# The S5 core of a fused block: four stages with a hand-made recurrence against one stage in four chunks with a scan instruction

## Chip, core and metric
One core of one Trainium2 chip. The metric is the device time of one execution, in microseconds (us); less is better. The engines are TensorE (PE: matmuls; PEld: its weight loads), VectorE (DVE), ScalarE (ACT), GpSimd (POOL) and SyncE (SP), which here only issues DMAs. They run their own instruction queues and meet at semaphores.

## What is computed
A gated delta net, a dense FFN, an S5 mixer, a mixture of experts and two attention layers on 512 tokens of width 1024. The change lies in the S5 mixer alone:
```python
def s5_mixer(x, w_in, lam_re, lam_im, log_dt, b_re, b_im, c_re, c_im, d_skip, w_glu):
    u = (x @ w_in).astype(f32)
    lam = lax.complex(lam_re, lam_im); dt = jnp.exp(log_dt)[:, None]
    a_bar = jnp.exp(lam * dt)
    b_bar = ((a_bar - 1.0) / lam)[..., None] * lax.complex(b_re, b_im)
    # h_t = a_bar * h_(t-1) + b_bar u_t   for 64 groups of 16 features, 64 complex states each
    # y_t = real(c h_t) + d_skip * u_t
    hid = jax.nn.gelu(y, approximate=False)
    val, gate = jnp.split(hid @ w_glu, 2, axis=-1)
    return val * jax.nn.sigmoid(gate)
```
(The two comment lines stand for the reference's chunked associative scan.)

## The kernel before
Names: P is 128, STEP 8 tokens, NJ = 64 blocks of 8 tokens, PAIRS = 32 pairs of groups (one of the pair in partitions 0 to 63, the other in 64 to 127), GC = 16 features of a group. The recurrence runs over the 64 blocks; inside a block of 8 tokens everything is matrices. A `Stage` gives each engine its own list of instructions; the next stage begins when all engines are through.

`s5_u` (`s5_project`, L1951): the projection x @ w_in in eight feature groups f. ScalarE rounds weight tiles (`split_hi`), VectorE makes their low parts (`split_lo`, L3858, two inputs from SBUF), and TensorE multiplies in three passes (`three_pass`, L263 to L267); ScalarE copies each group out (L1984), stores it to DRAM (L1989), and SP loads it back with tokens turned into blocks (`load_turned`, L1948, 8 DMAs a group, into `u_blk`). Beside that VectorE builds the matrices from inputs to block states (`powers`: 48 operations of 512 elements, L2085 to L2096, into `p_t`), three powers ahead of the low part of tile 2, two ahead of that of tile 3, three behind. GpSimd has nothing.

`s5_tables` (L2014): 64 transposes of `p_t` (L2036), copied to `into`, then the block inputs (L2045), copied to `e_all`.

`s5_scan` (L2167): VectorE steps eight blocks of eight with one complex product a step (L2266 to L2270), then carries between the eight (L2277 to L2281), then adds the carried part (L2294 to L2298). GpSimd clears three mixing buffers (L2319) and makes powers of the pole (`block_powers`, L2154 to L2164, two-input operations while VectorE steps). SP loads the output matrices `q_re`, `q_im` (L2305, 16 DMAs), TensorE makes the responses inside a block (`lags`, L2208/L2209, each group by itself on 64 rows), ScalarE copies them (L2241), and SP places each shifted copy of them in the mixing matrices `mix` with 8 DMAs a quarter (L2313, 32 in all); TensorE applies them (`within`, L2220), and keeps itself busy (`keep_busy`, L194) in between.

`s5_outputs` (L2334): the states times `q` (L2356), added by VectorE to the rest (L2366). `s5_gelu` (L2370): y turned back (L2389), d_skip * u added by VectorE (L2405), gelu on ScalarE (L2419), rounding (L2422) and low part (L2399), with 18 kept-busy calls on TensorE (two passes of 384 columns each). Then `s5_glu` multiplies by w_glu in its own stage; its first four weight tiles are loaded behind `s5_scan`, into the ring that `mix` used.

## Time and profile before
| | |
|---|---|
| median of 3 runs | 2594.73 us (2594.63 to 2598.16) |
| the profiled execution | span 2590.5 us from first to last instruction; instructions 41313 |
| busy: PE, DVE, ACT, POOL | 2477.6 us (96%), 1739.2 (67%), 1051.9 (41%), 589.9 (23%) |
| mean granted clock of TensorE | 0.991 of full |
| S5 part | `s5_u` 836.5 to 886.4, core and gelu to 981.2, then `s5_glu` |

A profile row gives an engine, a line of the kernel, the operation, written tile <- read tiles, partitions x elements and a count. "idle before" with an arrow is time that the engine stood still just before and who ended it. The granted clock is a share of 2.4 GHz; at 0.5 TensorE runs at 1.2 GHz. Kept-busy matmuls count as busy.

### The profile page before, as it was taken

The numbers are of one execution on the slowest core, as the hardware profiler recorded it, in microseconds if no ns is written. First come the engines' busy times: TensorE is split into PE (matmuls) and PEld (weight loads), VectorE is DVE, ScalarE is ACT, GpSimd is POOL, SyncE is SP. The second block draws the span as 40 slices with busy tenths as digits, with TensorE's granted clock in tenths as the row PEclk, the third lists the DMA queues.
The fourth block names the chain that finished last, engine by engine and source line by source line (L and its number), as shares of the span: only waits on it lengthen the run. The fifth ranks groups of instructions, "written<-read, shape, count | busy, mean of one in ns | idle before, by whom it ended". The sixth has DMA issues, their size and how long they took to land. (4 is left out here: it accounts for less than half of the span.)

```text
span 2590.5 us, 41313 instructions
## 1 busy us (share of the span) xinstructions
PE 2477.6 (96%) x15961; PEld 2036.9 (79%) x15961; DVE 1739.2 (67%) x2869; ACT 1051.9 (41%) x1561; POOL 589.9 (23%) x447
## 2 busy tenths in 40 slices
PE   8998999999999989899999999998999999999998
PEld 6788887788887768899999999886776576767566
DVE  6945656467676784576666767676687567487667
ACT  4443233321212333355555555533344443344453
POOL 2404321430230020052333432440024001024001
PEclk9999999999999999999999999999999999999999
DMA  4321002346654252267776777853221211332121
GB/s 155 98 83 35 2 3 65 124 156 237 212 182 148 76 166 84 91 219 229 254 240 224 252 236 231 271 184 125 86 74 60 76 66 57 109 94 70 33 82 65
DMA packets 259968, 339.98 MB, mean 131 GB/s; under 512 B 24928, under 2 KB 217952, under 8 KB 259232
## 3 DMA queue, kind: packets, MB, share of 16 engines
q1 hardware_dynamic: 251840, 315.52, 37.6%
q0 software_dynamic: 4512, 15.99, 1.8%
q10 hardware_dynamic: 3456, 6.29, 0.8%
q8 instruction: 106, 1.74, 0.3%
q14 instruction: 54, 0.44, 0.1%
HBM read 318.63 MB, written 16.52 MB: 129 GB/s over the span
## 5 line engine op out<-in xcount | busy, mean ns | idle before, releaser
L3020 PE MATMUL ps<-x_feat_r,moe_w_hi 128*128 128x384 f32 x1408 | 405.1, 361 | 0.6 <-DVE x_feat_r L3132 0.6
L2545 DVE TENSOR_TENSOR moe_w_lo<-ring,moe_w_hi 128x2048 fp32r<-128x2048 f32 x144 | 316.1, 2196 | 126.8 <-ACT moe_w_hi L2540 126.6
L3023 PE MATMUL ps<-x_feat_r,moe_w_lo 128*128 128x192 f32 x1408 | 354.0, 251 | 0.0
L2540 ACT ACTIVATE moe_w_hi<-ring 128x2048 fp32r<-128x2048 f32 x144 | 254.8, 1770 | 93.5 <-PE ps L263 76.2
L3023 PEld LDWEIGHTS ps<-x_feat_r,moe_w_lo 128*128 128x128 f32 x1408 | 269.2, 191 | 0.3
L3020 PEld LDWEIGHTS ps<-x_feat_r,moe_w_hi 128*128 128x128 f32 x1408 | 264.3, 188 | 1.7 <-issue 1.4
L267 PE MATMUL ps<-x_free_r,ring_r 128*128 128x512 f32 x496 | 195.6, 394 | 0.0
L266 PE MATMUL ps<-ring_r,x_feat_r 128*128 128x256 f32 (+2 forms) x576 | 185.1, 321 | 0.0
L263 PE MATMUL ps<-x_feat_r,ffn_w_hi 128*128 128x512 f32 x352 | 139.3, 396 | 1.2 <-DVE ffn_w_lo L2488 1.2
L267 PE MATMUL ps<-x_feat_r,ffn_w_lo 128*128 128x512 f32 x352 | 139.4, 396 | 0.0
L266 PE MATMUL ps<-x_free_r,ffn_w_hi 128*128 128x512 f32 x352 | 138.5, 393 | 0.0
L2540 ACT ACTIVATE ffn_w_hi<-ring 128x2048 fp32r<-128x2048 f32 (+1 forms) x35 | 61.8, 1768 | 169.4 <-PE ps L263 100.8
L4061 ACT ACTIVATE s_sb<-s_sb,att_small 128x512 f32<-128x512 f32 (+3 forms) x128 | 71.9, 562 | 133.3 <-DVE att_small L4053 133.1
L266 PEld LDWEIGHTS ps<-ring_r,x_feat_r 128*128 128x128 f32 x576 | 110.0, 191 | 7.8
L194 PE MATMUL ps<-cst 128*128 128x384 f32 x266 | 95.4, 506 | 17.8 <-PEq L175 15.7
L267 PEld LDWEIGHTS ps<-x_free_r,ring_r 128*128 128x128 f32 x496 | 93.2, 188 | 21.2
L3068 ACT ACTIVATE moe_cross<-ps 128x384 f32<-128x384 f32 (+1 forms) x96 | 44.4, 462 | 150.5 <-PE ps L3023 150.5
L263 PE MATMUL ps<-x_feat_r,acc_r 128*128 128x512 f32 x256 | 102.2, 399 | 0.0
L267 PE MATMUL ps<-x_feat_r,ring_r 128*128 128x512 f32 x256 | 101.7, 397 | 0.0
L266 PE MATMUL ps<-x_free_r,acc_r 128*128 128x512 f32 x256 | 101.5, 397 | 0.0
L3251 POOL TENSOR_TENSOR moe_hid_hi<-moe_prod,cst 128x384 fp32r<-128x384 f32 (+1 forms) x48 | 54.3, 1131 | 190.2 <-DVE moe_prod L3195 190.2
L4329 POOL TENSOR_TENSOR sq<-c_all 128x512 f32<-128x512 f32 x16 | 19.7, 1234 | 341.7 <-ACT c_all L3937 341.7
(661 smaller groups left out, 6407.1 us busy)
## 6 DMA issues: line engine op xcount, KB each, us to landing
ring<-in_moe_w SPq DMA_DIRECT2D x120, 1024.0 KB, 5.5
ring<-in_w_in SPq DMA_DIRECT2D x32, 1024.0 KB, 5.3
ring<-in_ffn_w SPq DMA_DIRECT2D x30, 1024.0 KB, 7.4
ring<-in_ada_t SPq DMA_DIRECT2D x48, 512.0 KB, 4.3
ring<-in_gdn_w_in SPq DMA_DIRECT2D x12, 1024.0 KB, 6.0
ring<-in_moe_w SPq DMA_DIRECT2D x24, 512.0 KB, 3.8
ring<-in_s_w_glu SPq DMA_DIRECT2D x8, 1024.0 KB, 5.6
ring<-in_w_out SPq DMA_DIRECT2D x8, 1024.0 KB, 6.2
```

The costliest lines, as they stand in the source:

```text
L194: prog.nc.tensor.matmul(prog.ps[:, bank, 0:3 * P], prog.ident, prog.cst, start=True, stop=True)
L263: m = nc.tensor.matmul(out, lh, rh, start=first, stop=False)
L266: nc.tensor.matmul(out, lh, rl, start=False, stop=False)
L267: return nc.tensor.matmul(out, ll, rh, start=False, stop=last)
L2540: self.prog.nc.scalar.activation(self.flat(self.hi, j % SPLITS, j), self.raw(j), ACT.Copy).then_inc(self.hi_done, 1)
L2545: self.prog.nc.vector.tensor_tensor(self.flat(self.lo, j % SPLITS, j), self.raw(j), self.flat(self.hi, j % SPLITS, j).bitcast(F32), ALU.su ...
L3020: mm = nc.tensor.matmul(out, wh[:, k, cs], both[:, k, :], start=(k == 0), stop=False)
L3023: mm = nc.tensor.matmul(out[:, 0:SLOTS], wl[:, k, cs], xg[0][:, k, :], start=False, stop=(k == KD - 1))
L3068: nc.scalar.activation(cross_of(c, which), half(c, which, 1), ACT.Copy).then_inc(cross_copied, 1)
L3251: nc.gpsimd.tensor_tensor(hi, src, prog.ones[:, 0:1].unsqueeze(2).to_broadcast([P, len(ms), SLOTS]), ALU.mult).then_inc(hi_ready, 1)
L4061: self.nc.scalar.activation(x, x, ACT.Exp, bias=self.small[:, u % 4, 1:2], scale=self.heads[h][3], accum_out=self.small[:, u % 4, 2:3]).th ...
L4329: m = nc.gpsimd.tensor_tensor(sq[:, 0 if first else 1, :], c_all[:, k, :], c_all[:, k, :], ALU.mult)
```

## The change
- `s5_tables`, `s5_scan`, `s5_outputs` and `s5_gelu` become one stage, `s5_core`, that goes through the 32 pairs in four chunks of eight.
- The recurrence is turned into a frame that rotates with the pole's angle: what is left is a real decay, done by `tensor_tensor_scan` (two instructions of 128x512 a chunk). The rotations, for 63 blocks and 32 pairs, and the decays are made by GpSimd during `s5_u`, by doubling. VectorE turns the inputs into the frame and the states out of it (`scan`).
- The response matrices of both groups of a pair come out of one matmul over 128 rows, with weights that are zero outside their own group (`lag_w`, written by GpSimd). GpSimd adds the skip term to them, and SP places them with 16 DMAs a chunk, one set for each group, in four mixing buffers.
- `within` and `states` add up in PSUM; gelu reads PSUM. The projected features stand in a ring of three.
- The four weight tiles of `s5_glu` are loaded inside `s5_core`, one behind each chunk's output.

Cut to what matters, with the removed functions (printed above) left out:
```diff
-GSTEP = 8
+SC = 4
+SQ = PAIRS // SC
+QUAD = SQ // 2
+LR = 2 * GC
...
+        for part, table in enumerate((mag, cos, pow_im)):
+            m = nc.vector.tensor_copy(s5.pole[:, part, :], table[:, STEP, :])
+        link(m)
...
+class S5Room:
...
+    U_RING = 3
...
+        raw = new("raw", [P, 2 * PAIRS * (STEP + 1) * GC])
+        n = 2 * PAIRS * P
+        self.p_t = raw[:, 0:n].rearrange("p (r q i c) -> p r q i c", r=2, q=PAIRS, c=GC)
+        self.tmp = raw[:, n:n + 2 * PAIRS * GC].rearrange("p (r q c) -> p r q c", r=2, c=GC)
...
+        self.rot = new("rot", [P, 2, PAIRS, NJ])[:, :, :, :]
+        self.decay = new("decay", [P, PAIRS, NJ])[:, :, :]
+        work = new("work", [P, 4, 2 * SQ * NJ])
+        self.turn = [work[:, i, :].rearrange("p (q j) -> p q j", q=PAIRS) for i in range(4)]
+        self.e, self.t, *self.h = (work[:, i, :].rearrange("p (r q j) -> p r q j", r=2, q=SQ) for i in range(4))
...
+        self.into = [x.rearrange("p k n -> p (k n)").rearrange("p (q n) -> p q n", n=P) for x in (prog.x_feat, prog.x_free)]
+        self.hid = [self.u_ring[:, n].rearrange("p i j -> p (i j)") for n in range(self.U_RING)]
...
+def rotations(nc, link, s5, room):
+    tt = nc.gpsimd.tensor_tensor
+    rot, turn = room.rot, room.turn
+    nc.gpsimd.memset(rot[:, 0, :, 0], 1.0)
+    nc.gpsimd.memset(rot[:, 1, :, 0], 0.0)
+    for part in range(2):
+        nc.gpsimd.tensor_copy(rot[:, part, :, 1], s5.pole[:, 1 + part, :])
+    link(nc.gpsimd.tensor_copy(room.decay, s5.pole[:, 0, :].unsqueeze(2).to_broadcast([P, PAIRS, NJ])))
+    link(nc.gpsimd.memset(room.decay[:, :, 0], 0.0))
+    n = 1
+    while n < NJ - 1:
+        m = min(n, NJ - 1 - n)
+        shape = [P, PAIRS, m]
+        re, im = (rot[:, part, :, 1:m + 1] for part in range(2))
+        top_re, top_im = (rot[:, part, :, n:n + 1].to_broadcast(shape) for part in range(2))
+        t = [x[:, :, 0:m] for x in turn]
+        tt(t[0], re, top_re, ALU.mult)
+        tt(t[1], im, top_im, ALU.mult)
+        tt(t[2], re, top_im, ALU.mult)
+        link(tt(t[3], im, top_re, ALU.mult))
+        tt(rot[:, 0, :, n + 1:n + m + 1], t[0], t[1], ALU.subtract)
+        link(tt(rot[:, 1, :, n + 1:n + m + 1], t[2], t[3], ALU.add))
+        n += m
...
+def s5_project(prog, name, s5, room):
...
+        def u_feat(f):
+            return room.u_ring[:, f % room.U_RING]
...
+                if f >= room.U_RING:
+                    act.wait_ge(u_stored[f - room.U_RING], 16)
...
+            def powers(taus):
+                real_powers(prog, dve, link, bbar, pow_re, pow_im, by_step[0], taus, room.tmp)
+                imaginary_powers(prog, nc.vector, room.tmp, link, bbar, pow_re, pow_im, by_step[1], taus)
+            proj.split_lo(dve, 0)
+            proj.split_lo(dve, 1)
+            powers(BACK[0:3])
+            proj.split_lo(dve, 2)
+            powers(BACK[3:5])
+            proj.split_lo(dve, 3)
+            powers(BACK[5:])
+        @st.gpsimd
+        def _(pool):
+            rotations(nc, linker(pool, pool_link), s5, room)
...
+def s5_core(prog, name, s5, room):
...
+    jobs = [(b, r, 8 * b + 4 * half) for b in range(SC) for r in range(2) for half in range(2)]
+    T_BANKS = (2, 3, 4, 5, 6, 7)
+    by_dve = [i < 8 and i % 2 == 1 for i in range(len(jobs))]
...
+                pe.wait_ge(prog.u_landed[b], 2 * 16 * STEP)
+                for r in range(2):
+                    for n in range(SQ):
+                        q = b * SQ + n
+                        for gp in range(2):
+                            m = nc.tensor.matmul(ps[TOKENS[gp], E_BANK + r, n * NJ:(n + 1) * NJ],
+                                                 into[r][:, q, TOKENS[gp]], u_blk[:, PAIRS * gp + q, :], start=True, stop=True)
+                m.then_inc(e_ready, 1)
...
+                rows = lag_rows(s // 2)
+                for n in range(QUAD):
+                    q = s * QUAD + n
+                    out = ps[rows, LAG_BANK + s % 2, n * P:(n + 1) * P]
+                    for r, x in enumerate((q_re, q_im)):
+                        m = nc.tensor.matmul(out, room.lag_w[r][:, q, :], flat_steps(x[:, q, 0:STEP, :]),
+                                             start=(r == 0), stop=(r == 1))
...
+            def within(b):
+                pe.wait_ge(placed[b], 32 * STEP)
...
+            def states(b):
+                pe.wait_ge(h_ready, b + 1)
...
+                pe.wait_ge(y_copied, 2 * b + 2)
...
+            turn_tables(0)
+            turn_tables(1)
+            inputs(0)
+            turn_tables(2)
+            turn_tables(3)
+            lags(0)
+            lags(1)
+            inputs(1)
+            lags(2)
+            lags(3)
+            within(0)
+            states(0)
+            inputs(2)
+            lags(4)
+            lags(5)
+            turn_back(0)
+            within(1)
+            states(1)
+            inputs(3)
+            lags(6)
+            lags(7)
+            turn_back(1)
+            within(2)
+            states(2)
+            turn_back(2)
+            within(3)
+            states(3)
+            pe.wait_ge(e_read, SC)
+            keep_busy(prog, E_BANK, 4)
+            turn_back(3)
+            keep_busy(prog, E_BANK, 10)
...
+            def finish(b):
+                act.wait_ge(e_ready, 3 + b // 2)
+                for gp, f in enumerate(features(b)):
+                    n = 2 * b + gp
+                    hid = room.hid[n % room.U_RING]
+                    if n >= room.U_RING:
+                        act.wait_ge(lo_done, n - room.U_RING + 1)
...
+                        act.wait_ge(y_turned, 2 * b + half + 1)
+                        nc.scalar.activation(by_half[:, half],
+                                             ps[:, TURN_BANK + half, :].rearrange("p (i g j) -> p g i j", g=2, j=NJ)[:, gp], ACT.Gelu
+                                             ).then_inc(gelu_done, 1)
+                    act.wait_ge(gelu_done, 2 * n + 2)
+                    nc.scalar.activation(prog.x_hi[:, f, :], hid, ACT.Copy).then_inc(hi_done, 1)
...
+            def scan(b):
+                e, t, h = room.e, room.t, room.h[b % 2]
+                shape = [P, 2, SQ, NJ]
+                cos, sin = (rot[:, part, chunk(b), :] for part in range(2))
+                dve.wait_ge(e_ready, b + 1)
+                raw = ps[:, E_BANK:E_BANK + 2, :].rearrange("p r (q j) -> p r q j", j=NJ)
+                tt(e, raw, cos.unsqueeze(1).to_broadcast(shape), ALU.mult)
+                tt(t[:, 0], raw[:, 1], sin, ALU.mult)
+                m = tt(t[:, 1], raw[:, 0], sin, ALU.mult)
+                m.then_inc(e_read, 1)
+                dve.wait_ge(e_read, b + 1)
+                tt(e[:, 0], e[:, 0], t[:, 0], ALU.add)
+                link(tt(e[:, 1], e[:, 1], t[:, 1], ALU.subtract))
+                decay = room.decay[:, chunk(b), :].rearrange("p q j -> p (q j)")
+                for r in range(2):
+                    m = nc.vector.tensor_tensor_scan(t[:, r].rearrange("p q j -> p (q j)"), decay,
+                                                     e[:, r].rearrange("p q j -> p (q j)"), 0.0, ALU.mult, ALU.add)
+                link(m)
+                if b >= 2:
+                    dve.wait_ge(y_ready, 2 * (b - 2) + 2)
+                tt(e, t, cos.unsqueeze(1).to_broadcast(shape), ALU.mult)
+                late, early = slice(1, NJ), slice(0, NJ - 1)
+                tt(h[:, 0, :, late], t[:, 1, :, early], sin[:, :, early], ALU.mult)
+                link(tt(h[:, 1, :, late], t[:, 0, :, early], sin[:, :, early], ALU.mult))
+                tt(h[:, 0, :, late], e[:, 0, :, early], h[:, 0, :, late], ALU.subtract)
+                link(tt(h[:, 1, :, late], e[:, 1, :, early], h[:, 1, :, late], ALU.add))
+                dve.sem_inc(h_ready, 1)
...
+            tt(skip, mask.unsqueeze(1).to_broadcast(shape), s5.d_skip.unsqueeze(2).to_broadcast(shape), ALU.mult
+               ).then_inc(skip_ready, 1)
+            copy_tables(0)
+            copy_tables(1)
+            scan(0)
+            scan(1)
+            scan(2)
+            split_lo(0)
+            scan(3)
+            for b in range(1, SC):
+                split_lo(b)
...
+                pool.wait_ge(lag_copied, s + 1)
+                rows, qs = lag_rows(s // 2), slice((s % 2) * QUAD, (s % 2 + 1) * QUAD)
+                nc.gpsimd.tensor_tensor(room.lag[rows, qs, 0:GC], room.lag[rows, qs, 0:GC], skip[rows, qs, :], ALU.add
+                                        ).then_inc(skip_added, 1)
+                pool.wait_ge(skip_added, s + 1)
+            for r in range(2):
+                m = nc.gpsimd.memset(room.lag_w[r], 0.0)
+            link(m)
+            for gp in range(2):
+                rows = TOKENS[gp]
+                for r in range(2):
+                    link(nc.gpsimd.tensor_copy(room.lag_w[r][rows, :, gp * GC:(gp + 1) * GC], s5.bbar[rows, r]))
+            pool.sem_inc(wide_ready, 1)
+            pool.wait_ge(skip_ready, 1)
+            for b in range(SC):
+                zero(b)
+                add_skip(2 * b)
+                add_skip(2 * b + 1)
...
+            sp.wait_ge(prog.u_last_stored, 16)
+            load_turned(prog, sp, u_blk, KD - 1)
             for s in range(NS):
+                sp.wait_ge(turned, min(8 + 4 * (s // 2), len(jobs)))
+                for r, dst in enumerate((q_re, q_im)):
+                    sp.dma_start(dst[:, quad(s), :, :], prog.q_dram[:, r, quad(s)]).then_inc(q_landed[s], 16)
+            for b in range(SC):
+                sp.wait_ge(zeroed, b + 1)
+                sp.wait_ge(skip_added, 2 * b + 2)
+                for i in range(STEP):
+                    n = (STEP - i) * GC
                     for gp in range(2):
+                        at = LR * b + GC * gp
+                        sp.dma_start(mix[b][i * GC:(i + 1) * GC, :, gp, i * GC:], room.lag[at:at + GC, :, 0:n]
+                                     ).then_inc(placed[b], 16)
+            for b in range(SC):
+                sp.wait_ge(y_ready, 2 * b + 2)
+                W.load(sp, W.issued)
+                W.issued += 1
```

## Rows read from the trace of the kernel before
**Rows 1.** Stretches; busy us of PE, PEld, DVE, ACT, POOL; granted clock; DMA.
```profile
836.50:842.10 5.60, 5.58 (x11) 3.81 (x12) 4.08 (x5) 3.99 (x5) 0.00 (x0) 0.50 0.02 4
842.10:886.40 44.30, 42.60 (x186) 34.69 (x185) 36.82 (x51) 12.26 (x10) 0.00 (x0) 1.00 0.29 82
886.40:981.20 94.80, 79.97 (x1060) 65.82 (x1060) 75.47 (x130) 41.83 (x61) 20.00 (x27) 0.98 0.46 127
923.90:927.40 3.50, 3.50 (x35) 2.43 (x32) 3.31 (x10) 1.18 (x2) 0.00 (x0) 0.51 0.57 92
981.20:988.90 7.70, 6.21 (x29) 6.22 (x30) 4.79 (x5) 3.99 (x5) 0.00 (x0) 0.56 0.46 157
```
**Rows 2.** Timeline of PE, scan to glu: start, length.
```profile
922.92 1.09 PE L2220 MATMUL ps<-ring,s_ublk 128*64 128x128 f32 x16 [2.11 <-DMA ring<-ring]
...
942.73 1.97 PE L2220 MATMUL ps<-ring,s_ublk 128*64 128x128 f32 x32 [1.96 <-DMA ring<-ring]
...
967.73 11.78 PE L194 MATMUL ps<-cst 128*128 128x384 f32 x36
982.69 0.58 PE L263 MATMUL ps<-s_glu_hi,x_feat_r 128*128 128x256 f32 x1 [3.18 <-DVE ring_r L242]
```
**Rows 3.** Groups of one line: duration in ns min/median/max, first and last start.
```profile
L2036 PE MATMUL ps<-cst,s_he x64: 272/273/302, 886.6 to 893.5; 128*128 128x128 f32 x64
L2045 PE MATMUL ps<-s_ublk,s_into x256: 222/222/270, 893.7 to 901.2; 128*64 128x64 f32 x128
...
L2419 ACT ACTIVATE s_hid<-s_yfeat x8: 1122/1130/1164, 966.6 to 978.5; 128x512 f32<-128x512 f32 x8
L2422 ACT ACTIVATE x_feat_r<-s_hid x8: 629/630/633, 967.8 to 979.6; 128x512 fp32r<-128x512 f32 x8
...
909.69 1.06 ACT L2241 ACTIVATE ring<-ps 16x512 f32<-16x512 f32 x2 [8.12 <-PE ps L2209]
```
**Rows 4.** The timeline of DVE, PE and ACT in `s5_u`.
```profile
865.71 2.29 DVE L3858 TENSOR_TENSOR ring_r<-ring,acc_r 128x2048 fp32r<-128x2048 f32 x1 [0.25 <-ACT acc_r L3850]
873.44 0.39 PE L263 MATMUL ps<-x_feat_r,acc_r 128*128 128x512 f32 x1
879.52 0.69 DVE L2096 TENSOR_TENSOR s_he<-s_u_tmp 128x512 f32<-128x512 f32 x1
884.74 1.03 ACT L1984 ACTIVATE s_ufeat<-ps 128x512 f32<-128x512 f32 x1 [4.44 <-PE ps L267]
```
**Rows 5.** GpSimd's operations alone: two lines' groups, two rows of its timeline.
```profile
L1480 POOL TENSOR_TENSOR acc<-acc,gdn_ms 128x512 f32<-128x512 f32 x2 | 2.1, 1064 | 0.9 <-DVE gdn_ms L1486 0.9
L1482 POOL TENSOR_TENSOR acc<-acc,gdn_z 128x512 f32<-128x512 f32 x2 | 2.5, 1267 | 0.2
...
211.90 2.35 POOL L1679 TENSOR_TENSOR gdn_z<-gdn_z,gdn_par 128x1024 f32<-128x1024 f32 x1 [85.18 <-POOLq L175]
922.93 0.39 POOL L2164 COPY x_free<-x_free 128x256 f32<-128x256 f32 x1
```
**Rows 6.** Timelines of DVE and POOL, alone and against each other.
```profile
24.54 2.33 DVE L953 SCALAR_TENSOR_TENSOR gdn_ktok<-gdn_conv_padded,gdn_taps,gdn_ktok 128x512 f32<-128x512 f32 x3
71.58 4.00 DVE L953 SCALAR_TENSOR_TENSOR gdn_ktok<-gdn_conv_padded,gdn_taps,gdn_ktok 128x512 f32<-128x512 f32 x3
71.51 1.29 POOL L866 TENSOR_TENSOR gdn_z_hi<-gdn_vtok,gdn_z_hi 128x512 fp32r<-128x512 f32 x1 [3.11 <-ACT gdn_z_hi L914]
72.76 1.49 POOL L862 TENSOR_TENSOR gdn_vtok<-gdn_q 128x512 f32<-128x512 f32 x1
...
918.65 0.83 DVE L2269 TENSOR_TENSOR x_free<-x_free,s_he 128x512 f32<-128x512 f32 x1
```
**Rows 7.** SP's DMA groups: placement, turned loads and the latter's landing.
```profile
L2313 SPq DMA_DIRECT2D ring<-ring x32: 559/618/2565, 912.7 to 940.7; - x32
L1948 SPq DMA_DIRECT2D s_ublk<-u_turn x64: 303/431/1360, 849.4 to 891.2; - x64
...
DMA to landing us min/median/max: 1.7/1.9/2.9
```

546 lines of the change are left out of this document (196 added, 350 removed).

## The prediction
> **What bounds the kernel now.** I read the views in this order. The page's first part: TensorE is busy for 96% of the span. That share hides two kinds of time that a change of the S5 part can win: idle stretches, and matmuls that only keep the clock up. So I cut the span into stretches [rows 1]: the projection `s5_u` with its start at half clock (836.5 to 842.1) and the rest of it to 886.4, the four stages behind it (tables, scan, outputs, gelu) from 886.4 to 981.2, and the first 7.7 us of the gated projection behind them, again at 0.56 of the full clock. In the 94.8 us of the four stages TensorE shows 80.0 us busy, but that includes 34 kept-busy calls (68 passes of L194, of which the last 36 take 11.78 us [rows 2]); no engine is the limit of all four stages. In the scan stage VectorE goes through its hand-made recurrence (75.5 us of VectorE in the stretch [rows 1]), while TensorE waits for the placed matrices again and again [rows 2]; at the end ScalarE's gelu (1.12 us for each of eight features, then 0.63 us of rounding [rows 3]) is what TensorE idles for. The reader should see a chain that changes engine from stage to stage with nothing overlapped across the stage borders. In `s5_u`, by contrast, TensorE is the limit: VectorE has done its last power at 880.2, TensorE goes on to about 884.7, and ScalarE's copy behind it ends at 885.8 [rows 4], so VectorE has 6 us to spare.
>
> **Part 1, the rotations on GpSimd in `s5_u`.** GpSimd is idle there before (0.00 us busy [rows 1]). The change puts one copy of 128x2048 and 36 two-input operations there: six for each m of 1, 2, 4, 8, 16, 31, on 32m elements. Four of six read an operand that repeats along the innermost axis; the nearest row took 1.04 us for 512 elements, two full operands 1.27 us for 512 and 2.35 us for 1024 [rows 5]. That is 2.1 ns an element for two full operands over a start of 0.19 us, and 1.66 ns with a repeated one. Port time (I count 0.05 us of the start): m=31 (992 elements) 4x1.70 + 2x2.13 = 11.1 us; m=16 5.9; m=8 3.1; m=4, 2, 1 together 3.3; the copy, by 0.39 us for 256 elements [rows 5], 2.4. Sum 25.8 us.
> Is it hidden? GpSimd alone would have 49 us for it. But VectorE's operations there all read two inputs from SBUF, and where both do that, three of L953 take 4.00 us against L866 and L862 on GpSimd, and 2.33 us without them [rows 6]. 1.67 us of the about 2.1 us that the two hold the port (0.9 and 1.15 us, from the end of the VectorE instruction that they wait for) come on top, 80%. For small operations less: VectorE's 0.69 us become 0.83 beside GpSimd's operations of 128 elements (0.32 us of port time), 44%, since VectorE's own start hides the rest [rows 6]. So 0.8 x (11.1+5.9+3.1+2.4) + 0.4 x 3.3 = 19.3 us: VectorE ends at 880.2 + 19.3 = 899.5. TensorE meets it earlier: the low part of tile 3 was made at 865.7 to 868.0 [rows 4] and is needed at 873.4 [rows 4]; behind 30 slowed operations it comes at about 882, so TensorE stands still for some 9 us and ends the last two groups near 894 to 897. That is before 899.5, so it adds nothing more. The stage ends 899.9 instead of 886.4: **+13.5 to +14 us**, I take +14. Below: 0 if the port isn't shared by these operations; above: +20 if all 25.8 us come through.
> The Trainium skill, page "SBUF — State Buffer", section "Who interferes with whom", says that a VectorE instruction with two SBUF inputs and a GpSimd instruction that reads SBUF exclude each other for their whole length: "the other fully blocks". By that rule, the trace agrees [rows 6], and the whole sum is +20 instead of +14, the end at 2596. It speaks against this change, for GpSimd's work looks free in a table of busy shares.
>
> **Part 2, four stages become one.** The work of TensorE stays: 64 transposes in 6.9 us, the inputs' 256 passes in 7.6 us, each pass of 128 columns 0.055 us where two halves of the array run side by side (32 in about 1.8 us) [rows 2, 3]. Only the lag matmuls change form: 64 of them over all 128 rows with nothing beside them, two passes of 0.109 us each (the transposes' pace), 1.75 us for four pairs. VectorE's recurrence, which filled the scan stage, becomes four calls of scan(b): two operations of 1024 elements (about 1.22 us each, between 0.69 for 512 and 2.29 for 2048 [rows 4]), eight of 512 at 0.61 to 0.69, sum 7.7 us, and two of the scan instruction, which the trace doesn't show: 0.69 us as an ordinary two-input operation, up to 2 us when an element depends on the last. I take 1.2. It matters little: the first two calls are wanted 27 and 41 us into the stage and are done at 17 and 27, the last two begin when their inputs are there and have 17 us each. Only from 3 us an instruction on does VectorE set the end.
> A sentence on a page: the Trainium skill, "DVE: opcode table, instruction layouts, handler registers and perf-mode slots", section "Datapath and trigger behaviour", says that this instruction runs at half throughput; by it each is 1.2 us, 4 us in all beyond a two-input operation, none of it on the path.
> What sets the end is the chain lags, copy, skip addition, placement, within. The placement was 32 DMAs (median 0.62 us of SP each, 256 pieces) and becomes 64 of 128 pieces; the turned loads have 128 pieces and take 0.43 us, begun 0.475 us apart [rows 7]. I take 0.51 us between two, 8.2 us for a chunk's 16, and 2.2 us for the last to land (the turned loads: 1.9 in the middle, 2.9 at most [rows 7]). Working it out from the stage's start:
> (a) turn 16 tables 7.0, inputs(0) 1.9, lags(0), (1) 3.5: 12.4; TensorE comes from a pause, so the clock is at its lower level (1.2 GHz) for the first few us, +1.6: 14.0.
> (b) ScalarE's copy 0.53 (half of the old pair's 1.06 [rows 3]), GpSimd's addition of 64 elements about 0.4 (0.19 + 64 x 2.1 ns, and its semaphore): 15.1. SP has issued its 16 loads of q by then.
> (c) 16 placements 8.2 and landing 2.2: 25.5. TensorE did inputs(1), lags(2), (3) and then idles 5 us.
> (d) within 1.8, states 3.6, inputs 1.9, lags 3.5, turning back 0.9, within 1.8, states 3.6, inputs 1.9, lags 3.5: 22.5, to 48.0; half clock behind the idle 5 us, +2.2: 50.2.
> (e) copy, addition 1.1, 16 placements 8.2, landing 2.2: 61.7; 7.2 us of TensorE's work (chunks 1 and 2) lie under it.
> (f) within(3) 1.8, states(3) 3.6, 4 kept-busy calls 2.6 (8 passes at 11.78/36 = 0.327 us), turning back 0.9, 10 calls 6.5: 15.4, and 1.7 for the clock: 78.8.
> The last ten calls outlast the gelu of the last chunk (four of 0.57, two roundings of 0.63, one low part of 0.69: about 5 us), which they cover. On SP nothing else waits behind the placements but the four loads of the next weights; three go out at about 58 us, the last behind states(3) at 67, and the first tile is there long before it is needed.
> So 78.8 us stand for 94.6: **-15.8**. Skip terms, table copies and the wait on the ring of three features cost nothing: ScalarE has 12 us of work in 44 in `s5_u` [rows 1], and the stored feature it waits for is two groups old. If the ring's cover were gone it would be the store's 2.2 us.
>
> **Part 3, the start of the next stage.** Before, TensorE's last kept-busy pass ended at 979.5 and the first matmul came 3.18 us later [rows 2], and the 7.7 us around it ran at 0.56 [rows 1], which costs 3 us. Now the kept-busy calls themselves end the stage, and the pause is 1.7 us. A pause of 1.96 us before 942.73 was followed by full clock, one of 2.11 us before 922.92 by 3.4 us at the lower level [rows 1, 2]. So I take **-3**; 0 is the other end.
>
> **Sum.** 14 - 15.8 - 3 = -4.8 us on the profiled span of 2590.5; the median of the runs, 2594.73, lies 4.2 us above that span, and nothing changes around it. 2594.73 - 4.8 = 2590.
>
> **The rivals.** (A) GpSimd's work is hidden. For it: GpSimd has 49 us for 26, and some VectorE inputs repeat along the innermost axis, as in no row here. Against: [rows 6]. The 14 us fall away: 2576. (B) The placement on SP sets a slower beat. The old 32 were begun between 912.7 and 940.7 [rows 7], 0.9 us apart with their waits; if the 64 go at 0.9 too, the 32 on the path add 32 x 0.39 = 12.5 us: 2602. From 0.66 us between two the kernel is no faster than before, from 0.82 it is slower by what can be measured. For it: each chunk's matrices move as many small pieces as before, and the first meet the q loads. Against: 0.475 us apart for the same count of pieces. (C) The port passes on everything: +6, 2596. (D) The clock does not fall in the core: -5.9, 2584; against it, two pauses of 3 and 5 us. (E) The scan instruction doesn't do what it is for and takes 4 us, so VectorE becomes the bound: +9, 2599; against it, no two-input row is near this.
>
> **How the numbers follow.** Forecast 0.38 (its own range 2585 to 2595), A 0.15, B 0.20, C 0.12, D 0.10, E 0.05. A measurement can tell about 0.2%, 5.2 us, from no change: faster is below 2589.5, slower above 2599.9. Faster: A, D and half of the forecast's chance, 0.44. Same: the other half and C, 0.31. Slower: B and E, 0.25. The range goes from just under A to B with a little more, 2574 to 2604.
>
> **What would show it.** In `s5_u`: L2085-like operations of 0.69 us grow to over 2 us beside GpSimd's widest ones, and TensorE waits some 9 us for VectorE at the sixth group; if they stay at 0.69, A holds. In the core: TensorE's wait for the placement DMAs, about 5 us before the first within and 3 us before the last; starts of placement DMAs 0.5 us apart; scan instructions near 1.2 us; the granted clock at 1.0 at the start of the gated projection. The prediction is wrong if the stage behind `s5_u` starts before 890, or the core takes under 72 or over 86 us.

## The result and the profile after

The changed kernel takes 2600.5 us in the median of nine runs against 2594.6 for the kernel before, a ratio of 1.0026 with a 95% interval of 1.0015 to 1.0038: slower by 3.9 to 9.9 us, best value 6.7. The forecast was 2590, a little faster; the time lies in its range (2574 to 2604), its direction is wrong: 4.8 us less were forecast. The profiled execution of the changed kernel took 2603.47 us with a span of 2601.8.

Windows of the changed kernel, cut where its stages and waits are (columns as in [rows 1]):

```profile
839.00:842.00 3.00, 2.94 (x5) 1.25 (x5) 2.30 (x2) 2.96 (x5) 2.84 (x8) 0.50 0.04 8
842.00:876.30 34.30, 34.23 (x144) 27.84 (x144) 33.75 (x31) 10.05 (x9) 33.52 (x30) 0.96 0.25 72
876.30:891.40 15.10, 0.00 (x1) 0.03 (x1) 14.96 (x7) 1.02 (x1) 12.73 (x6) 0.58 0.18 46
891.40:906.60 15.20, 13.30 (x48) 10.45 (x49) 11.67 (x18) 2.14 (x2) 0.03 (x1) 0.86 0.11 32
906.60:935.50 28.90, 18.78 (x256) 17.57 (x256) 23.48 (x34) 8.76 (x16) 12.20 (x13) 0.90 0.66 205
935.50:961.00 25.50, 25.46 (x392) 23.94 (x392) 14.67 (x19) 8.71 (x14) 4.19 (x4) 0.91 0.30 48
961.00:975.30 14.30, 7.81 (x115) 6.93 (x114) 9.19 (x12) 8.49 (x15) 0.92 (x1) 0.96 0.28 44
975.30:993.80 18.50, 18.42 (x132) 13.80 (x132) 1.39 (x2) 4.54 (x8) 0.00 (x0) 0.85 0.71 228
993.80:1002.00 8.20, 6.60 (x55) 6.60 (x56) 4.79 (x5) 4.00 (x5) 0.00 (x0) 1.00 0.43 147
```

TensorE has three stretches with long idle times: all of 876.3 to 891.4 in the projection, and in the core (906.6 to 993.8) some 10 of the first 28.9 us and 6.5 of the 14.3 us before 975.3. The timeline of TensorE says what ended each (start, length, instruction, in brackets the idle time before it and its releaser):

```profile
891.40 0.77 PE L263 MATMUL ps<-x_feat_r,acc_r 128*128 128x512 f32 x1 [15.17 <-DVE ring_r L3895]
...
906.62 3.68 PE L2181 MATMUL ps<-cst,s_raw 128*128 128x128 f32 x32 [1.91 <-PEq L175]
...
935.54 3.68 PE L2228 MATMUL ps<-ring,s_ublk 128*64 128x128 f32 x32 [8.21 <-DMA ring<-acc]
939.15 4.13 PE L2240 MATMUL ps<-s_raw,s_work 64*64 64x128 f32 x64
...
949.86 1.97 PE L2228 MATMUL ps<-ring,s_ublk 128*64 128x128 f32 x32
...
975.28 3.68 PE L2228 MATMUL ps<-ring,s_ublk 128*64 128x128 f32 x32 [5.03 <-DMA ring<-acc]
...
995.40 0.38 PE L263 MATMUL ps<-s_glu_hi,x_feat_r 128*128 128x256 f32 x1 [1.68 <-DVE ring_r L242]
```

L2228 is `within`, L2240 `states`, L2181 the turning of the tables. From such rows of both kernels the two spans compare like this (us):

| stretch | before | after | difference | forecast |
|---|---|---|---|---|
| start of the span to the first kept-busy matmul of `s5_u` | 836.5 | 839.1 | +2.5 | 0 |
| `s5_u`, to the first turned table | 50.1 | 67.6 | +17.5 | +14 |
| four stages, or the core, to the last kept-busy pass | 92.9 | 87.1 | -5.8 | |
| pause before the gated projection | 3.2 | 1.7 | -1.5 | |
| (these two together, forecast) | | | -7.3 | -15.8 |
| first 200 matmuls of the gated projection | 26.7 | 24.0 | -2.7 | -3 |
| the rest | | | +1.3 | 0 |

The S5 part alone comes to +7.5 us, which lies inside what the medians show (3.9 to 9.9). The first and the last line are not the change's: `s5_u` began between 836.0 and 839.6 us in the executions of all kernels below, which are alike up to there, and what follows the start of the gated projection took between 1602.9 us (experiment 10) and 1611.7 us (experiment 6) in the changed kernels. So every experiment is read from its own stages first and from its median second. One of the five executions of experiment 3 ran at a granted clock of 0.636 and took 3525.8 us, and is left out of its ratio.

### The profile page after: what moved, and what is told of

It is laid out like the page before. It is cut to its first block and busy times, and to the rows that moved or that the text cites. A ratio compares the mean times of both kernels' runs of the same rounds, so it can differ in the third digit from the quotient of the medians.

```text
span 2601.8 us, 40981 instructions
## 1 busy us (share of the span) xinstructions
PE 2470.5 (95%) x15793; PEld 2034.8 (78%) x15793; DVE 1732.9 (67%) x2804; ACT 1040.5 (40%) x1553; POOL 635.1 (24%) x480
## 5 line engine op out<-in xcount | busy, mean ns | idle before, releaser
L263 PE MATMUL ps<-x_feat_r,acc_r 128*128 128x512 f32 x256 | 102.5, 400 | 15.2 <-DVE ring_r L3895 15.2
L194 PE MATMUL ps<-cst 128*128 128x384 f32 x226 | 83.6, 517 | 15.5 <-PEq L175 13.4
```

The lines of the kernel that those rows point to most:

```text
L194: prog.nc.tensor.matmul(prog.ps[:, bank, 0:3 * P], prog.ident, prog.cst, start=True, stop=True)
L263: m = nc.tensor.matmul(out, lh, rh, start=first, stop=False)
```

## The experiments

Every kernel was compared with the kernel before on the same chip, whose median was 2594.4, 2595.3, 2594.9 and 2595.9 us in the four groups of runs. "Projection" is `s5_u` from its first kept-busy matmul to the core's first turned table (before 50.1, after 67.6), "core" from there to the last kept-busy pass (after 87.1).

**1. No rotations.** The table of rotations is filled with 1 and 0; the work of the other engines stays.

```diff
-    n = 1
-    while n < NJ - 1:
...
-        n += m
+    nc.gpsimd.memset(rot[:, 0], 1.0)
+    nc.gpsimd.memset(rot[:, 1], 0.0)
```

> This kernel is the changed one without the 36 two-input operations of the rotations on GpSimd: the table is filled with 1 and 0 by two memsets, so the states come out in a wrong frame; everything else stays, the copy of the decay too. Theory P (the 17.5 us that the projection stage grew, 67.6 us between its first kept-busy matmul and the core's first transpose where it was 50.1, are VectorE and GpSimd excluding each other): the stage goes back to 50 to 51 us, VectorE's power operations back to 0.69 us, the whole to 2600.5 - 17 = 2583.5. Rival R (the stage grew because of something else in it, such as the ring of three stored features or the moved low part of tile 3): GpSimd's absence changes little, the stage stays above 60 us, the whole within 3 us of 2600. Both: the core stays at 87 us.

Measured: 2582.2 us, ratio 0.9952 (0.9936 to 0.9969). The projection takes 50.2 us, the core 86.9. The whole growth of the projection is the rotations' doing, and with it gone the rest of the change is worth 12 us.

**2. The rotations alone, in the kernel before.**

```diff
+            @st.gpsimd
+            def _(pool):
+                rotations(nc, linker(pool, pool_link), pole, room)
```

> This kernel is the one before with the same rotations (36 two-input operations, the copy of 2048 elements) on GpSimd in its projection stage, on operands of the same shapes, into memory that nothing reads. Theory P: the stage grows by 17 us (50.1 to about 67), TensorE stops some 15 us before the last quarter of the weights, the whole is 2594.6 + 17 = 2612. Rival R: GpSimd's work is not what does it, the stage stays within 3 us of 50.

Measured: 2614.7 us, ratio 1.0070 (1.0049 to 1.0091), so +18 us, as much as the first experiment took away. The projection takes 67.5 us, and TensorE stops where it does in the changed kernel, for the same wait:

```profile
888.54 0.77 PE L263 MATMUL ps<-x_feat_r,acc_r 128*128 128x512 f32 x1 [15.27 <-DVE ring_r L3897]
...
903.66 0.52 PE L2075 MATMUL ps<-cst,s_he 128*128 128x128 f32 x3 [1.89 <-PEq L175]
...
1003.16 0.38 PE L263 MATMUL ps<-s_glu_hi,x_feat_r 128*128 128x256 f32 x1 [3.19 <-DVE ring_r L242]
```

In the projection it is 17.4 us less there and 17.4 us more here: the cost hangs on GpSimd's work and on nothing else of the change. The four stages behind it took 96.3 us here and 92.9 in the kernel before, which no experiment explains. The last row shows one thing more: the pause before the gated projection is 3.19 us, as in the kernel before (3.18), and yet the next 7.7 us ran at a granted clock of 1.00 where they ran at 0.60 there; the first 200 matmuls took 24.0 us, as in the changed kernel.

**3. One operand in PSUM.** The same work on both engines; only where VectorE's operands live is changed.

```diff
-    pow_re, pow_im, bbar = s5.pw[:, 0], s5.pw[:, 1], s5.bbar
+    pow_re, pow_im = s5.pw[:, 0], s5.pw[:, 1]
+    bbar, first = (prog.ps[:, b:b + 2, :].rearrange("p r (q c) -> p r q c", c=GC) for b in (4, 6))
+    tmp = (first[:, 0], room.tmp[:, 1])
...
             proj.split_hi(act, 0)
+            for r in range(2):
+                nc.scalar.activation(bbar[:, r], s5.bbar[:, r], ACT.Copy).then_inc(moved, 1)
             proj.split_hi(act, 1)
```

> The changed kernel with the operand that all of VectorE's powers read (bbar) copied into two PSUM banks by two ScalarE copies, and the first of the two temporaries in PSUM too, so that each of the 48 power operations has one SBUF and one PSUM input; GpSimd's rotations stay. Theory P (only a VectorE instruction with two SBUF inputs excludes GpSimd): power operations stay near 0.7 us beside GpSimd, only the low parts of tiles 2 and 3 collide, the stage is 50 to 54 us instead of 67.6, the whole 2600.5 - 15 = 2585. Rival P' (any work of GpSimd on SBUF slows VectorE, wherever its operands are): power operations of 1.5 to 2.5 us beside the wide rotations as now, the whole within 3 us of 2600.

Measured: 2582.0 us, ratio 0.9941 (0.9922 to 0.9959); the projection takes 50.1 us. VectorE and GpSimd in the changed kernel, with the widest rotations beside the powers:

```profile
874.95 2.40 DVE L2103 TENSOR_TENSOR s_raw<-s_bbar,s_pow 128x512 f32<-128x512 f32 x1
877.38 2.27 DVE L2104 TENSOR_TENSOR s_raw<-s_raw 128x512 f32<-128x512 f32 x1
876.76 2.34 POOL L2006 TENSOR_TENSOR s_work<-s_rot 128x992 f32<-128x992 f32 x1
...
886.36 2.74 POOL L2010 TENSOR_TENSOR s_rot<-s_work 128x992 f32<-128x992 f32 x1
886.98 4.27 DVE L3895 TENSOR_TENSOR ring_r<-ring,acc_r 128x2048 fp32r<-128x2048 f32 x1
891.17 0.68 DVE L2093 TENSOR_TENSOR s_raw<-s_bbar,s_pow 128x512 f32<-128x512 f32 x1
```

and in this kernel:

```profile
867.74 0.70 DVE L2107 TENSOR_TENSOR ps<-ps,s_pow 128x512 f32<-128x512 f32 x1
868.35 0.68 DVE L2108 TENSOR_TENSOR s_raw<-ps,s_pow 128x512 f32<-128x512 f32 x1
869.79 3.44 DVE L3900 TENSOR_TENSOR ring_r<-ring,acc_r 128x2048 fp32r<-128x2048 f32 x1
...
867.27 1.93 POOL L2006 TENSOR_TENSOR s_work<-s_rot 128x992 f32<-128x992 f32 x1
...
871.03 3.98 POOL L2008 TENSOR_TENSOR s_work<-s_rot 128x992 f32<-128x992 f32 x1
```

The reader should see three things. In the changed kernel each of VectorE's 512-element operations lasts about as long as the GpSimd operation beside it (2.27 and 2.40 against 2.34), and is back at 0.68 as soon as GpSimd is done. With one input in PSUM the two engines run at their own speeds, 0.70 and 1.93. And where VectorE still reads two SBUF inputs, for the low part of a weight tile (L3900), the two collide as before: 3.44 instead of 2.29 there, 3.98 instead of 1.93 on GpSimd. So it is not GpSimd's activity that slows VectorE but two operands of VectorE in SBUF. The Trainium skill, page "SBUF — State Buffer", section "Who interferes with whom", says that a VectorE instruction with at most one SBUF input, outside its two-port modes, doesn't contend with GpSimd; the trace agrees, 0.70 us beside GpSimd's 1.93.

**4. Placements on two queues.**

```diff
-            for b in range(SC):
-                sp.wait_ge(zeroed, b + 1)
...
+            for b in range(SC):
+                place(sp, b, 0)
...
+            copy_lags(0)
+            copy_lags(1)
+            place(act, 0, 1)
+            copy_lags(2)
+            copy_lags(3)
+            place(act, 1, 1)
             copy_y(0)
```

`place(eng, b, gp)` waits for the chunk's memset and skip additions and issues its eight DMAs of group gp; chunks 2 and 3 likewise behind `copy_lags(5)` and `(7)`.

> The changed kernel with the placements of one of the two groups of each pair issued by ScalarE instead of SP, 8 of a chunk's 16 each; the same DMAs, pieces and bytes. Theory Q (the core is longer than forecast because SP begins a placement only every 0.645 us, 11 to 12 us a chunk with one longer one in it): a chunk is issued in about 6 us, TensorE's waits before the first and the last within shrink from 8.2 and 5.0 us to about 2.5 and 0, the core from 87 to 77 us, the whole to 2590. Rival Q' (what takes the time is the landing of many small pieces on the DMA engines): both waits stay within 2 us of what they are, and the landing times grow.

Measured: 2601.8 us, ratio 1.0024 (1.0010 to 1.0038), core 85.3: next to nothing, and neither theory holds throughout. A chunk was issued in 6.5 us, about as theory Q had it. But the first chunk's placements landed late, as rival Q' had it, and TensorE's wait before the first within was still 6.9 us; the last chunk's did not land late, and the wait for them was gone (line view of the placements in each stretch):

```profile
L2179 SPq DMA_DIRECT2D ring<-acc x8: 596/636/1146, 919.0 to 924.5; - x8
L2179 ACTq DMA_DIRECT2D ring<-acc x8: 622/638/1492, 919.0 to 924.9; - x8
...
DMA to landing us min/median/max: 4.7/6.3/7.0
```
```profile
L2179 SPq DMA_DIRECT2D ring<-acc x8: 586/613/1424, 958.8 to 964.4; - x8
...
DMA to landing us min/median/max: 1.9/2.7/3.4
```

And ScalarE, busy issuing for 6.6 us, came late with its copies: TensorE now waited for it, 4.50 us, before the turning back that precedes the last within.

```profile
970.06 1.94 PE L2264 MATMUL ps<-cst,acc 128*128 128x128 f32 x8 [4.50 <-ACT acc L2319]
971.93 3.28 PE L2237 MATMUL ps<-ring,s_ublk 128*64 128x128 f32 x32
```

The last chunk had been placed by 966.7, 7.9 us after its first issue (12.4 in the changed kernel). The issue time saved on SP was given back as a wait for ScalarE.

**5. All lags first.**

```diff
             inputs(1)
-            lags(2)
-            lags(3)
+            for s in range(2, NS):
+                lags(s)
             within(0)
             states(0)
             inputs(2)
-            lags(4)
-            lags(5)
             turn_back(0)
```

> The changed kernel with the lag products of chunks 2 and 3 (and ScalarE's copies of them) moved ahead of the first within, into the 8.2 us in which TensorE waits for the first placement; the same instructions otherwise. Theory Q (the rest of the core is paced by SP: 64 placement DMAs at 0.645 us with one longer one in each chunk, 0.70 us apart on the mean; they stop at 945 to 951 and 961 to 963 only because the lags of chunks 2 and 3 come late): SP issues all 64 in one run of 45 us from the first, within(3) starts 5.5 us earlier, and as TensorE pauses less, within and states run at full clock; the core from 87 to 80 us, the whole 2600.5 - 7 = 2593.5. Rival L (the placements are limited by landing on the DMA engines, which the denser issue doesn't help): landing times grow past 4 us in chunks 1 to 3 and the core stays within 2 us of 87.

Measured: 2594.4 us, ratio 1.0004 (0.9993 to 1.0015); core 80.6 us. SP's queue now holds one unbroken run of placements where the changed kernel's covers 51 us with two holes:

```profile
922.87 51.13 SPq L2454 DMA_DIRECT2D ring<-acc  x64
```
```profile
921.58 44.88 SPq L2446 DMA_DIRECT2D ring<-acc  x64
```
```profile
957.56 1.97 PE L2228 MATMUL ps<-ring,s_ublk 128*64 128x128 f32 x32 [2.90 <-DMA ring<-acc]
...
967.73 3.68 PE L2228 MATMUL ps<-ring,s_ublk 128*64 128x128 f32 x32 [2.71 <-DMA ring<-acc]
```

64 DMAs in 44.88 us are 0.70 us each, and within(1), (2) and (3) all wait for them (0.49, 2.90 and 2.71 us): the pace of the core is the rate at which SP begins placements. The placements of chunks 1 to 3 landed in 1.8 to 2.9 us, no later than in the changed kernel. Rival L falls. One thing expected did not come: within(3) did not run at full clock but in 3.68 us.

**6. The q loads out of the way.**

```diff
-            for s in range(NS):
+            load_q(sp, range(NS // 2))
...
+            copy_lags(0)
+            copy_lags(1)
+            place(act, 0, 1)
+            copy_lags(2)
+            copy_lags(3)
+            load_q(act, range(NS // 2, NS))
```

> The changed kernel with chunk 0's 16 placements shared by SP and ScalarE (8 each) and the loads of q for chunks 2 and 3 (8 of 16 DMAs, 2.3 of 4.6 MB) issued by ScalarE behind them instead of by SP ahead of them; chunks 1 to 3 are placed by SP alone as in the changed kernel. In the run with two queues the placements of chunk 0 landed 4.6 to 7.0 us after their issue, and those of chunk 3 1.9 to 3.4 us. Theory T (that is because they stand behind the q loads on the DMA engines): now they land in 2 to 3.5 us, the first within starts about 21 us into the core instead of 28.9 (two queues with the q loads ahead: 26.6), TensorE's wait before it falls from 8.2 to under 2 us, the core to 80 us and the whole to 2593. Rival U (two queues beside each other are slow in landing whatever else runs): landing stays at 5 to 7 us, the first within at 26 us or later.

Measured: core 81.9 us, first within 24.0 us into it instead of 28.9, behind a wait of 3.2 us (under 2 was expected); the placements of chunk 0:

```profile
L2185 SPq DMA_DIRECT2D ring<-acc x8: 599/606/892, 921.2 to 926.1; - x8
L2185 ACTq DMA_DIRECT2D ring<-acc x8: 622/641/873, 921.2 to 926.4; - x8
...
DMA to landing us min/median/max: 2.2/3.0/3.8
```

Same two queues, same beat, 3.0 us to land instead of 6.3: theory T holds for the landing, and rival U falls. In chunk 1, which now follows the moved loads, the first placements took up to 6.7 us, the same effect once more. TensorE's wait before the last within was 6.1 us (5.0 in the changed kernel). The step to 21 us was missed by 3: at 24.0 the last landing (928.8) is bound by 5.9 us of issue and 2.4 of landing behind an addition at 921.1 that lies 16.4 us into the core, later than I had counted with. The median, 2599.1 (ratio 1.0011, 0.9996 to 1.0026), shows only 1.4 us of the 5 us that the core is shorter; the intervals allow 5.

The Trainium skill, page "DMA: Bandwidth & Descriptors", section "Issuing engines are not separate DMA queues", says that issuing from several engines at once saves only the time to initiate each, "which is usually small relative to the DMA itself". The first half is what experiments 4 and 6 show. The second doesn't hold for this row of small ones: in the changed kernel initiating takes 0.60 us each, 16 in a row 10.8 to 11.6, and the last one lands 1.8 us after it is begun (3.4 in chunk 1).

**7. Kept busy in the waits.**

```diff
             def within(b):
+                if b in (0, 3):
+                    pe.wait_ge(e_read, min(b + 2, SC))
+                    keep_busy(prog, E_BANK, 12 if b == 0 else 7)
                 pe.wait_ge(placed[b], 32 * STEP)
```

> The changed kernel with kept-busy calls (12 before the first within, 7 before the last) in TensorE's two long waits for the placement. Theory C (those two pauses cost, beside their own length, what runs behind them at the lower clock: within 3.68 where 1.97 us is had at full clock, states 4.13 and 4.72 where 3.71 is): the granted clock stays at 1.0 through the core, within(0) and within(3) take 1.97 us, the core 87 to 82 us, the whole 2600.5 - 5 = 2595.5. Rival (the clock falls at other places or on its own): within stays above 3 us.

Measured: granted clock 1.00 over the whole core and within back at 1.97:

```profile
905.90:988.10 82.20, 78.01 (x930) 64.70 (x930) 48.74 (x66) 30.54 (x53) 17.16 (x18) 1.00 0.53 146
```
```profile
926.25 8.01 PE L194 MATMUL ps<-cst 128*128 128x384 f32 x24
934.92 1.97 PE L2231 MATMUL ps<-ring,s_ublk 128*64 128x128 f32 x32 [0.66 <-DMA ring<-acc]
```

The core takes 82.2 us, 4.9 less than in the changed kernel (0.90 on the mean there): theory C holds. The median is 2598.9 (ratio 1.0015, 1.0004 to 1.0026); as in 6 the medians are too coarse to show 5 us.

**8. Experiments 3 and 5 together.**

> Both edits together: bbar and one temporary in PSUM (which gave 50 us for the projection stage), and all lag products ahead of the first within. If the two costs are in series and independent, the gains add up: 2600.5 - 18 - 7 = 2575.5, 0.7% below the kernel before. If the core's gain depends on the state that the projection leaves (clock, the last low part), it is nearer to 2582.

Measured: 2572.9 us, ratio 0.9923 (0.9906 to 0.9939); projection 50.1, core 77.2. The gains add up. The core is 3.4 us shorter than in 5: its first placement is begun 15.4 us after its start (16.0 in 5), and TensorE's four waits for placements sum to 7.8 us instead of 9.7.

**9. Six kept-busy calls at the end instead of ten**, on top of 8.

```diff
-            keep_busy(prog, E_BANK, 10)
+            keep_busy(prog, E_BANK, 6)
```

> The kernel with bbar in PSUM and all lags first (core 77.2 us there), with 6 kept-busy calls behind the last turning back instead of 10. In its trace VectorE ends the stage's work at 962.3 and the kept-busy calls at 964.93. Theory C (the pause in front of the next stage is the stage's own exchange of 1.7 us, whatever ends the stage): the next stage begins 2.6 us earlier, still at full clock; the whole 2573 - 2.6 = 2570.4. Rival: without the last calls TensorE's pause grows to 3 us or more and the start of the next stage runs at half clock (it cost 3 us in the kernel before): 2573 or later.

Measured: 2572.0 us, ratio 0.9912 (0.9895 to 0.9928); core 76.0, pause 1.68. The next stage starts at full clock all the same:

```profile
964.80:972.50 7.70, 7.61 (x63) 7.61 (x64) 4.14 (x5) 2.68 (x3) 0.00 (x0) 1.00 0.46 157
```

The four calls are worth 2.6 us by their own rows, of which 1.2 came out; the waits for placements were 1.6 us longer here (3.06 and 2.96 us before within(1) and (3) where 8 had 0.76 and 1.77, 0.61 before within(2) where it had 2.54). That those calls are not needed for the clock is shown; their gain is not, against the medians.

**10. A quarter of the placements on ScalarE**, on top of 9.

```diff
+                place(sp, b, range(STEP - 2 if b else STEP))
...
             for s in range(NS):
                 copy_lags(s)
+            for b in range(1, SC):
+                place(act, b, range(STEP - 2, STEP))
             copy_y(0)
```

> As e9, with the last 4 of the 16 placements of chunks 1, 2 and 3 issued by ScalarE between its last lag copy and its first copy of y, where it stood idle for 7.7 us; chunk 0 is placed by SP alone. Theory Q (SP's beat of 0.70 us a placement paces within(1), (2) and (3), where TensorE waited 0.8, 2.5 and 1.8 us): SP's run shortens from 45 to 37 us, the three waits go, TensorE's own chain is the limit; 5 us less than e9, 2565.5. Rival: the 12 DMAs on ScalarE (7.7 us) push back its copy of y and the wait comes back in front of the turnings back: within 1.5 us of e9.

Measured: 2567.5 us, ratio 0.9891 (0.9875 to 0.9908), the fastest of all: 1.1% faster than the kernel before, 1.3% faster than the changed one. The core takes 70.2 us, 5.8 less than in 9.

```profile
901.42 38.12 SPq L2185 DMA_DIRECT2D ring<-acc  x52
```
```profile
915.15 2.45 PE L2243 MATMUL ps<-ring,s_ublk 128*64 128x128 f32 x32 [3.03 <-DMA ring<-acc]
...
925.34 1.97 PE L2243 MATMUL ps<-ring,s_ublk 128*64 128x128 f32 x32
...
941.31 1.97 PE L2243 MATMUL ps<-ring,s_ublk 128*64 128x128 f32 x32
945.66 3.71 PE L2255 MATMUL ps<-s_raw,s_work 64*64 64x128 f32 x64 [2.38 <-DVEq L2392]
```

Only the first within still waits for a placement; the last wait is now for VectorE's last scan. Here ScalarE issues in time that it had free, unlike in 4.

**11. Placement through DRAM.**

```diff
+                for gp in range(2):
+                    sp.dma_start(home[:, :, gp, :], room.lag[at:at + GC, :, :]).then_inc(lag_stored, 16)
+                sp.wait_ge(lag_stored, 32 * (b + 1))
                 for i in range(STEP):
-                    for gp in range(2):
-                        sp.dma_start(mix[b][i * GC:(i + 1) * GC, :, gp, i * GC:], room.lag[at:at + GC, :, 0:n])
+                    sp.dma_start(mix[b][i * GC:(i + 1) * GC, :, :, i * GC:].rearrange("c q g n -> c (q g) n"),
+                                 home[:, :, :, 0:n].rearrange("c q g n -> c (q g) n")).then_inc(placed[b], 16)
```

> The changed kernel with each chunk's copied lags stored to DRAM first (2 DMAs of 16 rows) and placed from there by 8 DMAs of 256 pieces instead of 16 of 128 from SBUF; the same bytes in SBUF. It tells what makes a placement take 0.60 us of SP where the turned loads, from DRAM and also of 128 pieces, take 0.43. Theory S (a source in SBUF is what makes it dearer): 0.43 us each even with 256 pieces; a chunk takes 0.9 + 2.2 (store landing) + 3.8 + 1.9 = 8.8 us instead of 12.6, the core 79.5 us instead of 87, the whole 2593. Theory N (the number of pieces counts): 0.62 us or more each; 10 us or more a chunk, the core 82 us, 2595.5. Rival: the extra landing eats the gain, core at 86 us or more.

Measured: 2600.4 us, ratio 1.0021 (1.0011 to 1.0030), core 84.4.

```profile
L2457 SPq DMA_DIRECT2D ring<-lag_turn x32: 308/608/1597, 927.1 to 968.9; - x32
...
DMA to landing us min/median/max: 2.2/3.2/4.0
```

From DRAM, 256 pieces took 0.61 us to begin, and the first of each chunk, whose rows join into 16 pieces of 8 KB, 0.31 to 0.35 (the minimum of the row); 128 pieces from DRAM take 0.43 ([rows 7]). So with a source in DRAM the number of pieces counts, as theory N says, and theory S falls in its form. But from SBUF, 128 pieces (0.60) and 256 ([rows 7], 0.62) cost the same. What makes 128 pieces from SBUF dearer than from DRAM is not settled. In time the core lies between theory N (82) and the rival (86): the last chunk was placed in 10.5 us instead of 12.4, but the first took 13.5, because its two stores landed only after 5.3 and 6.0 us, behind the q loads (2.3 to 3.4 in the other chunks).

**12. The last low part sooner.**

```diff
             proj.split_lo(dve, 2)
-            powers(BACK[3:5])
             proj.split_lo(dve, 3)
-            powers(BACK[5:])
+            powers(BACK[3:])
```

> The changed kernel with the low part of the last weight tile made before the fourth and fifth powers instead of behind them; GpSimd's rotations and all else stay. In the changed kernel TensorE stood still for 15.2 us for that low part, ended at 904.7 (ScalarE's copy at 905.8), 1.3 us after VectorE's last power (903.45). Theory: VectorE and GpSimd share the same sum of port time, so VectorE still ends at 64.4 us into the stage; TensorE is done long before, the stage is 2.3 us shorter (65.3 instead of 67.6) and ends with VectorE, but TensorE comes out of a pause of some 15 us right at the start of the core, whose first 32 transposes then take about 7 us at the lower clock instead of 3.7: whole 2600.5 - 2.3 + 3 = 2601, no change. Rival: TensorE's stop was what made the stage long, and it falls to under 60 us, the whole to 2593.

Measured: 2599.0 us, ratio 1.0011 (1.0002 to 1.0021); projection 66.0.

```profile
902.37 5.63 PE L2180 MATMUL ps<-cst,s_raw 128*128 128x128 f32 x32 [17.84 <-PEq L175]
```

TensorE's stop in the middle is gone, the stage is 1.5 us shorter (2.3 were expected) and ends with VectorE, 65.5 us into it. The core's first tables take 2.0 us more at the lower clock (5.63 against 3.68), but the lags behind them wait for the q loads anyway, and the core as a whole takes 86.4 us. So the 15 us pause of TensorE was a symptom; what VectorE and GpSimd cost each other sets the stage. The rival (under 60 us) falls.

## Why the prediction was wrong

Two steps failed: a wait of TensorE in part 1, and above all the beat of the placements in part 2.

**Part 1, the rotations (+14 forecast, +17.5 measured).** The mechanism was right, and rival A falls: experiments 1 to 3 show it from three sides. VectorE's work was lengthened by 20.7 us (its last power ends 64.4 us into the stage, 43.7 before [rows 4]), where I had 19.3 (80% of the wide operations' port time, 40% of the small ones'): a small error. It is 80% of the estimated 25.8 us, so rival C's condition, that all of it comes through, did not hold. The step that failed is the one behind it, "TensorE stands still for some 9 us and ends the last two groups near 894 to 897 ... so it adds nothing more". It stood still for 15.2, because the low part that it waited for sat behind GpSimd's longest operations (2.3 to 2.7 us each) and was itself stretched from 2.29 to 4.27; I had put it behind an average slowdown. TensorE ended at 904.7, 1.3 us behind VectorE, and ScalarE's copy 1.1 us behind that. Of the 3.5 us missed, experiment 12 gives 1.5 to this order; the rest is the sum itself and ScalarE's copy behind it. The words "the other fully blocks", which the prediction quotes from the Trainium skill's page "SBUF — State Buffer", section "Who interferes with whom", stand there for VectorE's two-port modes; for two SBUF inputs that page says that the instruction contends with a GpSimd instruction that reads SBUF, and calls the shared ports an exclusive lock. The trace shows nearly that: 2.3 us where 0.69 and 1.93 would be 2.6 one behind the other.

**Part 2, the core (78.8 forecast, 87.1 measured; -15.8 and -7.3).** By its own steps, in us from the core's start:

| step | forecast | measured |
|---|---|---|
| (a) second lags done | 14.0 | 15.0 |
| (b) skip added | 15.1 | 16.2 |
| (c) chunk 0 placed | 25.5 | 28.9 |
| (d) last lags done | 50.2 | 54.4 |
| (e) chunk 3 placed | 61.7 | 68.7 |
| (f) end | 78.8 | 87.1 |

The mis-sized term is the beat of the placements in (c) and (e): 0.51 us taken, 0.72 and 0.70 measured (0.64 between most, and one of 1.2 to 2 us in each chunk; no run shows what makes that one long). I had taken it near the turned loads because both have 128 pieces; the placement kept the 0.60 us that its predecessor with 256 pieces had [rows 7]. From the first issue to the last landing it makes 12.6 us in (c) and 12.4 in (e) where 10.4 was forecast, 4.2 of the 8.3 us. The prediction had the point at which this decides ("from 0.66 us between two the kernel is no faster than before"), and gave it to rival B with 0.20: B was right in mechanism, at 0.70 instead of 0.9. Experiment 5 shows that the beat paces the core, 10 that taking placements off SP gives 5.8 us. The remaining 4.1 are, by the steps, 0.2 in (b) and (c) and:
- 1.0 in (a). The first lags wait 1.9 us for q loads, which SP begins only 5.2 us into the core, behind the turned loads of the last feature, and the passes took 0.7 more; against that, the 1.6 us for the lower clock charged there did not come (3.68 us for 32 tables).
- 2.1 in (d) and (f). The two pauses were longer than forecast (8.2 and 5.0 us instead of 5 and 3), and the lower clock behind them cost 4.9 us in all (experiment 7) where I had 3.9; the rest lies in the passes themselves.
- 0.8 in (e), mostly GpSimd's addition, which took 0.92 us there where I had 0.4. VectorE did a scan instruction beside it, whose inputs both lie in SBUF; with VectorE idle the same addition took 0.31:

```profile
922.48 0.31 POOL L2422 TENSOR_TENSOR acc<-acc,s_pow 32x64 f32<-32x64 f32 x1 [2.56 <-ACT acc L2301]
...
961.86 0.92 POOL L2422 TENSOR_TENSOR acc<-acc,s_pow 32x64 f32<-32x64 f32 x1 [1.01 <-ACT acc L2301]
```

**What was right.** VectorE never bounds the core: a scan instruction takes 1.2 us (2.42 for two), the value taken, and rival E falls. The clock does fall in the core (0.90 on the mean), against rival D. The ring of three stored features costs nothing: without the rotations' price the projection is back at 50.2 and 50.1 us (experiments 1 and 3).

**Part 3 (-3 forecast, -2.7 measured): right in number, its reason not shown.** The gated projection starts at full clock behind a pause of 1.7 us. But in experiment 2 it did so too behind a pause of 3.19 us, with the old stages in front of it. So the shorter pause need not be what kept the clock up, and the 2.7 us may be no gain of the change; what lowered the clock in the kernel before stays open.

**The sum.** +17.5 - 7.3 - 2.7 is +7.5 where +14 - 15.8 - 3 was forecast. Two terms missed by 3.5 and 8.5 us, both upward. The miss of part 2 alone turns the sign (-4.8 + 8.5 = +3.7), that of part 1 alone does not (-1.3), nor do the beat's 4.2 us alone (-0.6). The forecast and B were treated as alternatives with fixed prices; they are one continuous quantity (the beat), and the row nearest in kind, the same queue's old placement at 0.62 us, should have had the middle of it.

## What to carry to other kernels

An idle GpSimd was not free here beside a VectorE whose instructions read two SBUF operands: each then took nearly the sum of both times (2.3 us for 0.69 and 1.93). Before moving work there, put one of VectorE's operands in PSUM, if banks are free, or find a stretch where VectorE reads one. Many small DMAs in a row on the critical path cost their issue time each (0.60 us here, for 8 KB as for 64 KB): take it from the queue's own row for the same kind of source and destination, keep the queue fed early (all producers first), and give a part to an engine that is idle at that moment, not to one that the chain needs next.

## What the runs showed that was not expected

- VectorE's instruction lasts as long as GpSimd's beside it (0.69 becomes 2.27 to 2.40 beside 2.34), and vice versa (1.93 becomes 3.98 beside a low part that takes 2.29 alone): near exclusion for two SBUF inputs, none with one input in PSUM (0.70).
- A placement within SBUF takes SP 0.60 us with 128 pieces and 0.62 with 256; a load from DRAM 0.31 with 16, 0.43 with 128, 0.61 with 256.
- Small DMAs issued from two queues right behind 4.6 MB of loads landed after 4.7 to 7.0 us instead of 1.9 to 3.4, on either queue; with 2.3 MB of these loads moved away, after 2.2 to 3.8. From one queue, where the later ones are begun later, the first took 5.2 us and the last 1.8.
- The length of a pause does not alone say what clock follows it: in the core of experiment 5 within ran in 1.97 us behind a pause of 2.90 us and in 3.68 behind one of 2.71; and the gated projection began at full clock behind 3.19 us in experiment 2 and at the lower one behind 3.18 us in the kernel before.
